# Attention items joined to 512 columns, one compressed item for all groups, and the output projection begun inside the last items

## The chip, the cores and the metric

The kernel runs on one core of a Trainium2 chip. The metric is device microseconds (us) for one execution, the median of several.

## The reference, cut to what matters

Three transformer layers run one after the other on 512 tokens of width 1024, all in float32. The third layer mixes two branches, a gated recurrence (`hgrn2`) and sparse attention (`nsa`), and only `nsa` and the projection behind it are touched here.

```python
# q: 2 kv groups G x 4 query heads R x 512 tokens x 64
s = einsum('bgrtd,bgnd->bgrtn', q, k_cmp) * scale          # 31 compressed keys
p_cmp = softmax(where(cvalid, s, NEG)) * any_valid
o_cmp = einsum('bgrtn,bgnd->bgrtd', p_cmp, v_cmp)
...                                                        # o_slc: keys k_s, causal
...                                                        # o_win: keys k_w, causal
o = gates[..., 0:1]*o_cmp + gates[..., 1:2]*o_slc + gates[..., 2:3]*o_win
mix = concatenate([o_hg, o_nsa]) @ w_out
x = x + gt1 * mix
```

With 512 tokens, 8 blocks and 16 to be selected, the selected branch is plain causal attention, and so is the window branch.

## The kernel before, in words

Every engine has its own program, and semaphores order them; `at(engine, stage, ...)` is the count that an earlier `tick(...)` of the same name reached. The stage of this change is "nsa". It begins with norms and rotations of seven chunks of queries and keys (`ss`, `rotate`; `NORMED` lists the chunks), with the compression of keys and values into 31 (`compress`, 64 products of 62 x 256, then "hidT" and "cmp2"), and with the half of the output projection that needs only `hgrn2` (`ahead(n)`, eight blocks of four 128x512 products, added to the residual by `dve_ahead`).

Then comes the item loop. `ITEMS` lists 36 items: for each query head r (0 to 3; both kv groups g go together) the compressed branch (b = 0), then for b = 1 and 2 the four 128-row query blocks i, each with (i + 1) x 128 keys. Per item TensorE computes scores, transposes the probabilities, and multiplies with the values:

```python
for n, (r, b, i) in enumerate(ITEMS):
    if n + 2 < len(ITEMS):
        scores(n + 2)          # L3466, compressed L3462
    for g in range(NG): ...    # transposes of item n: L3503, compressed L3501
    if n:
        values(n - 1)          # L3482, compressed L3478
```

VectorE runs `front(n + 1)` (masking and row maxima, L3611; compressed L3600 to L3606) and then the scaling of item n (reciprocal of the sum and gate, L3660 and L3664; compressed L3649 to L3656). ScalarE runs `exp(n + 1)` (L3547) and then copies the transposed probabilities of item n from PSUM to SBUF (L3562, L3560). VectorE copies the finished output of a head (`dve_o`, L3683 and L3684). Score banks alternate between the pairs (0, 1) and (6, 7); `scores(n + 2)` waits for `exp(n)`, the transposes of item n wait for its scaling, and `values(n)` for the copies.

Behind the loop `pe_mix_out` does the second half of the output projection, for the left 256 tokens (c = 0) and then the right (c = 1), eight blocks n of four 128x256 products each (L486); it begins only when every engine has ended the stage before (`begin`). VectorE adds each block to the residual (`residual`, L564). The up-projection of the feed-forward net (L675) and the down-projection (L759) follow until the end. Weights come through a ring of slots of 2 MB, loaded by SyncE when TensorE has `used` a slot.

Of the kernel before, what the change touches and what calls it, by code (L numbers as in the profile page):

```python
# [90 lines left out]
def program(nc, dr, out, plan):  # L91
# [3 lines left out]
    with ExitStack() as ctx:  # L95
# [28 lines left out]
        def at(*name):  # L124
            return plan.get(name, 1)
# [350 lines left out]
        def pe_mix_out(pe):  # L476

            tag = "mix_out"
            begin(pe, "pe", tag)
            for c, cols in enumerate(HALVES):  # L480
                for n in range(KC):
                    if n >= 2:
                        pe.wait_ge(dve_done, at("dve", tag, "res", c, n - 2))
                    bank = B[6 * c + n % 2]
                    for k in range(4, KC):
                        last = nc.tensor.matmul(bank[:, cols], out_weights(pe, tag, n, k), HT[:, k, cols], start=(k == 4), stop=(k == KC - 1))  # L486
                    last.then_inc(pe_done, PE.tick(tag, "proj", c, n))
                    if c == 1 and n == 1:
                        pe_mix_sums(pe, 0)
            used((tag, 1))  # L490

# [61 lines left out]

        def dve_mix_out(dve):
# [4 lines left out]

            def residual(c, n):  # L560

                cols = HALVES[c]
                dve.wait_ge(pe_done, at("pe", tag, "proj", c, n))
                nc.vector.scalar_tensor_tensor(out=XT[:, n, cols], in0=B[6 * c + n % 2][:, cols], scalar=mod[:, 2, 16 + n:17 + n], in1=XT[:, n, cols],  # L564
                                               op0=ALU.mult, op1=ALU.add).then_inc(dve_done, DV.tick(tag, "res", c, n))
# [19 lines left out]
            for n in range(KC):  # L585
                residual(0, n)
                if n == 4:
                    first()
                if n == 6:
                    second()  # L590
                add_square(0, n)
            dve_combine(dve, 5, 2, 32, 24, None)
            for n in range(KC):
                residual(1, n)
                if n >= 3:
                    normed(0, n - 3)
                add_square(1, n)
# [2755 lines left out]
        HID = region(o, 4, 2 * NCMP); o += 8 * NCMP  # L3353
        assert o <= 4 * HH * T
# [11 lines left out]
        ITEMS = [(r, b, i) for r in range(4) for b, i in [(0, 0)] + [(b, i) for b in (1, 2) for i in range(NT)]]  # L3366
# [8 lines left out]
        def pe_nsa(pe):  # L3375
# [45 lines left out]
            for n in range(LAST):  # L3421
                ss(n + 1)
                compress(12 * n, 12 * n + 6)
                if n in MIX_AHEAD:
                    ahead(MIX_AHEAD[n])
                rotate(n)
                compress(12 * n + 6, 12 * n + 12)
# [11 lines left out]
            pe.wait_ge(dve_done, at("dve", "nsa", "rotated", LAST - 1))  # L3439
            ahead(KC - 1, 0, 2)  # L3440
            pe.wait_ge(act_done, at("act", "nsa", "hid"))
            for g in range(NG):
                blk = slice(g * NCMP, (g + 1) * NCMP)
                for hc in range(2):
                    nc.tensor.matmul(B[4][half(g), 0:NCMP], w2c[:, 0, hc, :], HID[:, hc, blk], start=(hc == 0), stop=(hc == 1))
                for hc in range(2):
                    last = nc.tensor.matmul(B[5][0:NCMP, g * ND:(g + 1) * ND], HID[:, 2 + hc, blk], w2c[:, 1, hc, :],
                                            start=(hc == 0), stop=(hc == 1))
            last.then_inc(pe_done, PE.tick("nsa", "cmp2"))
            rotate(LAST)  # L3450

            def scores(n):

                r, b, i = ITEMS[n]
                if n == 0:
                    pe.wait_ge(act_done, at("act", "nsa", "cmp2"))
                if n >= 2:
                    pe.wait_ge(act_done, at("act", "nsa", "exp", n - 2, 1))
                if b == 0:
                    for i in range(NT):  # L3460
                        for g in range(NG):
                            last = nc.tensor.matmul(B4[SB[n % 2][g]][:, i, 0:NCMP], NX[half(g), r, i * P:(i + 1) * P], KCMP[half(g), 0:NCMP],  # L3462
                                                    start=True, stop=True)
                else:
                    for g in range(NG):
                        last = nc.tensor.matmul(B[SB[n % 2][g]][:, 0:(i + 1) * P], NX[half(g), r, i * P:(i + 1) * P],  # L3466
                                                NX[half(g), 5 + b, 0:(i + 1) * P], start=True, stop=True)
                last.then_inc(pe_done, PE.tick("nsa", "score", n))

            def values(n):  # L3470

                r, b, i = ITEMS[n]
                pe.wait_ge(act_done, at("act", "nsa", "pt", n, 1))
                if b == 0:
                    if r:
                        pe.wait_ge(dve_done, at("dve", "nsa", "o", r - 1))
                    for g in range(NG):
                        last = nc.tensor.matmul(B[4 + g][half(g), :], VCMP[0:NCMP, g, :], PTn[n % 2][0:NCMP, g, :], start=True, stop=True)  # L3478
                else:
                    for j in range(i + 1):  # L3480
                        for g in range(NG):
                            last = nc.tensor.matmul(B[4 + g][half(g), i * P:(i + 1) * P], VSW[:, j, (b - 1) * P + g * ND:(b - 1) * P + (g + 1) * ND],  # L3482
                                                    PTn[n % 2][:, g, j * P:(j + 1) * P], start=False, stop=True, skip_group_check=True)
                last.then_inc(pe_done, PE.tick("nsa", "pv", n))

            scores(0)
            scores(1)
            ahead(KC - 1, 2, 4)
            for n, (r, b, i) in enumerate(ITEMS):
                if n + 2 < len(ITEMS):  # L3490
                    scores(n + 2)
                for g in range(NG):
# [6 lines left out]
                    for j in range(NT if b == 0 else i + 1):  # L3499
                        if b == 0:  # L3500
                            last = nc.tensor.transpose(B4[2 + g][0:NCMP, j, :], Pn[n % 3][:, 4 * g + j, 0:NCMP], ident[:, :])  # L3501
                        else:
                            last = nc.tensor.transpose(B4[2 + g][:, j, :], Pn[n % 3][:, 4 * g + j, :], ident[:, :])  # L3503
                    last.then_inc(pe_done, PE.tick("nsa", "pt", n, g))
                if n:
                    values(n - 1)
            values(len(ITEMS) - 1)
            PE.mark("end", "nsa")

        def act_nsa(act):  # L3510
# [10 lines left out]
            for kv in (1, 0):  # L3521
# [6 lines left out]
            act.wait_ge(pe_done, at("pe", "nsa", "cmp2"))  # L3528
            nc.scalar.activation(KCMP[:, 0:NCMP], B[4][:, 0:NCMP], ACT.Copy).then_inc(act_done, AC.tick())
            nc.scalar.activation(VCMP[0:NCMP, :, :], B[5][0:NCMP, 0:2 * ND].rearrange("p (g d) -> p g d", g=2), ACT.Copy)\  # L3530
                .then_inc(act_done, AC.tick("nsa", "cmp2"))

            def exp(n):

                r, b, i = ITEMS[n]
                if n >= 3:
                    act.wait_ge(pe_done, at("pe", "nsa", "pt", n - 3, 1))
                if b == 0:
                    for g in range(NG):
                        act.wait_ge(dve_done, at("dve", "nsa", "max", n, g))  # L3540
                        nc.scalar.activation(Pn[n % 3][:, 4 * g:4 * g + 4, 0:NCMP], B4[SB[n % 2][g]][:, :, 0:NCMP], ACT.Exp, scale=SCALE)\
                            .then_inc(act_done, AC.tick("nsa", "exp", n, g))
                else:
                    for g in range(NG):
                        act.wait_ge(dve_done, at("dve", "nsa", "max", n, g))
                        c = 2 * (n % 2) + g
                        nc.scalar.activation(Pn[n % 3][:, 4 * g:4 * g + i + 1, :].rearrange("p j c -> p (j c)"), B[SB[n % 2][g]][:, 0:(i + 1) * P],  # L3547
                                             ACT.Exp, scale=-1.0, bias=small[:, 20 + c:21 + c], accum_out=small[:, 40 + c:41 + c])\
                            .then_inc(act_done, AC.tick("nsa", "exp", n, g))

            exp(0)
            for n, (r, b, i) in enumerate(ITEMS):
                if n + 1 < len(ITEMS):
                    exp(n + 1)
                if n >= 2:
                    act.wait_ge(pe_done, at("pe", "nsa", "pv", n - 2))
                for g in range(NG):
                    act.wait_ge(pe_done, at("pe", "nsa", "pt", n, g))
                    if b == 0:
                        ins = nc.scalar.activation(PTn[n % 2][0:NCMP, g, :], B[2 + g][0:NCMP, :], ACT.Copy)  # L3560
                    else:
                        ins = nc.scalar.activation(PTn[n % 2][:, g, 0:(i + 1) * P], B[2 + g][:, 0:(i + 1) * P], ACT.Copy)  # L3562
                    ins.then_inc(act_done, AC.tick("nsa", "pt", n, g))
            AC.mark("end", "nsa")

        def dve_nsa(dve):
# [22 lines left out]
            cm = cmask[:, :, 0:NCMP]  # L3589
            valid = cmask[:, :, 31:32].rearrange("p i o -> p (i o)")  # L3590

            def front(n):

                r, b, i = ITEMS[n]
                dve.wait_ge(pe_done, at("pe", "nsa", "score", n))
                if b == 0:
                    S = [B4[SB[n % 2][g]][:, :, 0:NCMP] for g in range(NG)]
# [414 lines left out]
```

## Time and profile before

| | |
|---|---|
| time, median of 3 runs | 2637.63 us (2636.24 to 2637.93) |
| the profiled execution's own time | 2635.95 us |
| its span, first to last instruction | 2634.2 us |
| TensorE busy | 2573.3 us, 98% |
| VectorE, ScalarE busy | 1684.4 us (64%), 723.4 us (27%) |
| item loop, first score to last value | 2105.08 to 2199.47 us |

Times of the trace are us from the start of the span. A float32 product appears as two records (a transpose as one), so "x8" of products is four of them. The duration of one record holds its latency; what it costs in a row of others is read from start to start.

### The profile page before, as it was taken

Reading aid. Unit: us, or ns where it says so; the run is one execution under the profiler, and the core shown is the slowest. Engines: PE = TensorE matmul, PEld = TensorE weight load, DVE = VectorE, ACT = ScalarE, POOL = GpSimd, SP = SyncE. Lnnn points to the kernel's source line nnn. Section 1 sums busy time; section 2 is a strip of 40 time slices with the busy share of each in tenths; the row PEclk is TensorE's granted clock in tenths of the full one; section 3 lists DMA queues with packets and bytes.
Section 4 is the critical chain, followed back from the end, with each engine's and each line's share of the span. In section 5 each row is a group of like instructions: output and inputs, shape, how many; then the busy total and the mean of one; then the engine's idle time right before and its main releaser. Section 6 shows DMA issues by size and latency. Waiting matters only on the chain.

```text
span 2634.2 us, 32114 instructions
## 1 busy us (share of the span) xinstructions
PE 2573.3 (98%) x12546; PEld 2061.6 (78%) x12546; DVE 1684.4 (64%) x3035; ACT 723.4 (27%) x1408; POOL 256.2 (10%) x186
## 2 busy tenths in 40 slices
PE   7999999999999999999999999999999999999999
PEld 3888887588888878888888888885445457888888
DVE  3788886687766374555648777645375586666652
ACT  3455553311110022211103111004263365222200
POOL 1333331010000030000001000002121000000000
PEclk9999999999999999999999999999999999999999
DMA  8221311235434321122023454331021310122121
GB/s 348 98 83 73 132 72 65 96 128 192 169 134 155 134 76 68 65 72 96 33 97 128 160 192 153 130 118 67 32 82 64 128 65 33 65 96 96 66 89 54
DMA packets 26373, 276.95 MB, mean 105 GB/s; under 512 B 3688, under 2 KB 4584, under 8 KB 9200
## 3 DMA queue, kind: packets, MB, share of 16 engines
q1 hardware_dynamic: 23040, 269.11, 27.0%
q10 hardware_dynamic: 3184, 5.78, 0.7%
q8 instruction: 101, 1.65, 0.3%
q14 instruction: 48, 0.39, 0.0%
HBM read 272.77 MB, written 2.11 MB: 104 GB/s over the span
## 4 chain that ended last, share of the span: by engine, by line
PE 88%; DVE 7%; ACT 2%; DMA 1%; issue 1%; POOL 0%; SPq 0%; ACTq 0%; DVEq 0%; POOLq 0%
PE bank L675 29%; PE bank L759 15%; PE bank L2585 11%; PE bank L1449 5%; PE bank L2998 5%; PE bank L2371 4%; PE bank L419 3%; PE bank L2676 1%; PE bank L1593 1%; DMA arena<-w_ada 1%; DVE arena L1910 1%; PE bank L486 1%; PE bank L2991 1%; PE bank L1585 1%; PE bank L3466 1%
## 5 line engine op out<-in xcount | busy, mean ns | idle before, releaser
L675 PE MATMUL bank<-HT,ring 128*128 128x256 f32 x1056 | 248.1, 381 | 2.0 <-ACT HT L1091 2.0
L675 PE MATMUL bank<-arena,ring 128*128 128x256 f32 x1056 | 249.6, 380 | 0.0
L675 PE MATMUL bank<-arena 128*128 128x256 f32 x1056 | 249.5, 380 | 0.0
L675 PEld LDWEIGHTS bank<-HT,ring 128*128 128x128 f32 x1056 | 199.8, 190 | 33.7 <-issue 5.2
L675 PEld LDWEIGHTS bank<-arena,ring 128*128 128x128 f32 x1056 | 201.1, 190 | 26.8
L675 PEld LDWEIGHTS bank<-arena 128*128 128x128 f32 x1056 | 201.1, 190 | 26.8
L759 PE MATMUL bank<-arena,ring 128*128 128x256 f32 x936 | 206.9, 380 | 1.4 <-ACT arena L832 1.4
L759 PEld LDWEIGHTS bank<-arena,ring 128*128 128x128 f32 x936 | 177.8, 190 | 26.6 <-ACT arena L832 2.6
L1315 ACT ACTIVATE arena<-bank,ffc 128x512 f32<-128x512 f32 x66 | 51.3, 777 | 485.5 <-DVE bank L1221 485.5
L1120 POOL TENSOR_SCALAR XT<-XT,comb_v 128x512 f32<-128x512 f32 x32 | 50.1, 1577 | 1054.5 <-ACT HT L1091 657.3
L2998 PE MATMUL bank<-HT,ring 128*128 128x512 f32 x320 | 146.5, 598 | 0.5 <-ACT HT L1132 0.5
L1449 PE MATMUL bank<-arena,ring 128*128 128x256 f32 x512 | 130.1, 381 | 1.9 <-DVE arena L1968 0.8
L675 PE MATMUL bank<-HT,arena 128*128 128x256 f32 x528 | 125.6, 381 | 2.7 <-DVE arena L1276 2.6
L759 PE MATMUL bank<-arena 128*128 128x256 f32 x528 | 116.4, 379 | 0.0
L675 PEld LDWEIGHTS bank<-HT,arena 128*128 128x128 f32 x528 | 99.8, 190 | 18.7 <-DVE arena L1276 5.8
L2585 PE MATMUL bank<-arena,ring 128*128 128x256 f32 x512 | 112.7, 380 | 0.3 <-DVE arena L2791 0.3
L759 PEld LDWEIGHTS bank<-arena 128*128 128x128 f32 x528 | 100.6, 190 | 13.4
L2585 PEld LDWEIGHTS bank<-arena,ring 128*128 128x128 f32 x512 | 97.4, 190 | 15.1 <-issue 1.4
L394 DVE SCALAR_TENSOR_TENSOR arena<-ring,evec,arena 128x512 f32<-128x512 f32 x140 | 104.6, 747 | 2.6
L2998 PEld LDWEIGHTS bank<-HT,ring 128*128 128x128 f32 x320 | 57.4, 190 | 58.8 <-issue 56.7
L1231 DVE SCALAR_TENSOR_TENSOR arena<-bank,ffc,arena 128x511 f32<-128x511 f32 (+1 forms) x132 | 98.5, 746 | 3.5 <-ACT arena L1315 1.1
L1449 PEld LDWEIGHTS bank<-arena,ring 128*128 128x128 f32 x512 | 89.2, 191 | 11.5 <-DVE arena L1968 1.2
(514 smaller groups left out, 4598.7 us busy)
## 6 DMA issues: line engine op xcount, KB each, us to landing
ring<-w_ada SPq DMA_DIRECT2D x33, 2048.0 KB, 7.8
ring<-w_up SPq DMA_DIRECT2D x33, 2048.0 KB, 7.7
ring<-w_down SPq DMA_DIRECT2D x24, 1408.0 KB, 6.0
ring<-w_gdn SPq DMA_DIRECT2D x7, 2048.0 KB, 10.1
ring<-w_ret_qk SPq DMA_DIRECT2D x4, 2048.0 KB, 7.9
ring<-w_ret_v SPq DMA_DIRECT2D x4, 2048.0 KB, 7.9
ring<-w_ret_g SPq DMA_DIRECT2D x4, 2048.0 KB, 8.0
ring<-w_ret_out SPq DMA_DIRECT2D x4, 2048.0 KB, 7.9
```

Of the source, the lines that this page charges most:

```text
L394: ins = nc.vector.scalar_tensor_tensor(out=acc, in0=w[:, :, k, :], scalar=evec[:, e, k:k + 1], in1=acc, op0=ALU.mult, op1=ALU.add)
L419: ins = nc.tensor.matmul(B[bank][:, :], out_weights(pe, tag, n, k), src(k), start=(first and k == k0), stop=(last and k == k1 - 1))
L486: last = nc.tensor.matmul(bank[:, cols], out_weights(pe, tag, n, k), HT[:, k, cols], start=(k == 4), stop=(k == KC - 1))
L675: last = nc.tensor.matmul(out_, w[:, k, :], x[:, k, :], start=(first and k == 0), stop=(k == 3), skip_group_check=not first)
L759: last = nc.tensor.matmul(out_, w[:, k, :], x(k), start=(first and k == 0), stop=(k == KH2 - 1), skip_group_check=not first)
L1120: nc.gpsimd.tensor_scalar(XT[:, n, :], XT[:, n, :], comb_v[:, 2, n:n + 1], comb_v[:, 3, n:n + 1], ALU.mult, ALU.add)\
L1231: last = nc.vector.scalar_tensor_tensor(out=out_[:, m:], in0=src[:, 0:T - m], scalar=ffc[:, i, j, half, 2 - m:3 - m], in1=out_[:, m:], op0 ...
L1315: nc.scalar.activation(ffn_y[:, j % 2, :], up_bank(j)[:, :], ACT.Identity, scale=ffc[:, i, j, 0, 2:3], bias=ffc[:, i, j, 0, 3:4])\
L1449: last = nc.tensor.matmul(out_, w[:, k, :], x[:, k, :], start=(first and k == 0), stop=(k == 3), skip_group_check=not first)
L2371: last = nc.tensor.matmul(out_, w[:, k, :], x[:, k, :], start=(first and fresh and k == 0), stop=(k == 7), skip_group_check=not (first and ...
L2585: last = nc.tensor.matmul(out_, left, right, start=flag, stop=(k == 3), skip_group_check=not (first and fresh))
L2998: last = nc.tensor.matmul(bank[:, :], w[:, u, k, :], HT[:, k, :], start=(k == 0), stop=(k == KC - 1))
```

## The change

The item list is new: an item now has always 512 score columns. `FULL_1` and `FULL_2` are query block 3 with its 512 keys; a mixed item joins two parts in one bank, blocks 0 and 2 of one branch (`MIXED_1`, `MIXED_2`: 128 + 384 columns) or blocks 1 of both branches (`MIXED`: 256 + 256). That is 5 items a head. The compressed branch is one item for all four heads: each head and query block takes 31 of 32 columns, so that its probabilities are transposed as four full blocks per group; its values are kept at four partition offsets (`VCMP`, written by "cmp2" four times over). The values of the compressed branch still are one product per group and head. There are 21 items.

Around the loop: `scores(0)` stands before the last rotation and "cmp2", `scores(1)` and `ahead(7)` behind it; within the six steps of norms `rotate` stands before the whole of `compress`; ScalarE takes over one of the two output copies of a head; the left half of the last head's output is copied as soon as the items of blocks 0 to 2 are done, and the first two blocks of the left half of the projection stand before the last item's values, without a wait for the end of the stage.

```diff
-        ITEMS = [(r, b, i) for r in range(4) for b, i in [(0, 0)] + [(b, i) for b in (1, 2) for i in range(NT)]]
+        FULL_1, FULL_2 = ((1, 3, 0),), ((2, 3, 0),)
+        MIXED_1, MIXED, MIXED_2 = ((1, 0, 0), (1, 2, 1)), ((1, 1, 0), (2, 1, 2)), ((2, 0, 0), (2, 2, 1))
+        CMP = ("compressed",)
+        ITEMS = [(0, FULL_1), (0, MIXED_1), (None, CMP), (0, MIXED), (0, MIXED_2), (0, FULL_2)]
+        ITEMS += [(r, parts) for r in range(1, 4) for parts in (MIXED, MIXED_1, MIXED_2, FULL_1, FULL_2)]
+        LEFT_DONE = N_ITEMS - 3
...
+                if parts == CMP:
+                    pe.wait_ge(act_done, at("act", "nsa", "cmp2"))
                     for i in range(NT):
+                        for r in range(4):
+                            for g in range(NG):
+                                last = nc.tensor.matmul(cmp_scores(n, g)[:, 4 * i + r, :], NX[half(g), r, i * P:(i + 1) * P], KCMP[half(g), 0:NCMP],
...
+                    for b, i, o in parts:
...
+                if r and n == FIRST_OF[r]:
+                    pe.wait_ge(dve_done, at("dve", "nsa", "o", r - 1))
+                    pe.wait_ge(act_done, at("act", "nsa", "o", r - 1))
+                    compressed_values(r, True)
...
+            for n in range(N_ITEMS):
+                if n + 2 < N_ITEMS:
+                    if n == 1:
+                        pe.wait_ge(dve_done, at("dve", "nsa", "rotated", LAST))
+                    scores(n + 2)
+                turned(n)
                 if n:
                     values(n - 1)
-            values(len(ITEMS) - 1)
+            pe_mix_proj(pe, 0, 0)
+            pe_mix_proj(pe, 0, 1)
+            values(N_ITEMS - 1)
...
+                if r and n == FIRST_OF[r] + 1:
+                    act.wait_ge(pe_done, at("pe", "nsa", "pv", LAST_OF[r - 1]))
+                    copied(1, r - 1, slice(0, T)).then_inc(act_done, AC.tick("nsa", "o", r - 1))
+                if n == N_ITEMS - 1:
+                    act.wait_ge(pe_done, at("pe", "nsa", "pv", LEFT_DONE))
+                    copied(0, 3, HALVES[0])
+                    copied(1, 3, HALVES[0]).then_inc(act_done, AC.tick("nsa", "left"))
...
+                if n == 0:
+                    scaled(0)
+                    front(1)
+                    dve_ahead(dve, "mix_out", 2, KC - 1, MIX_BANK[KC - 1])
                 else:
-                    c = 40 + 2 * (n % 2)
...
+                    if n + 1 < N_ITEMS:
+                        front(n + 1)
+                    scaled(n)
```

TensorE's program between "hidT" and the loop: before, L419 is `ahead(7)` in two halves, L3445 and L3447 "cmp2", L3418 the last rotation, L3462 and L3466 the first scores.

```order
L3435 MATMUL bank<-ident,arena 128x62 x8
L419 MATMUL bank<-arena,ring 128x512 x2
L3445 MATMUL bank<-arena,w2c 64x31 x2
L3447 MATMUL bank<-w2c,arena 31x64 x2
L3445 MATMUL bank<-arena,w2c 64x31 x2
L3447 MATMUL bank<-w2c,arena 31x64 x2
L3418 MATMUL bank<-arena,rot 128x512
L3462 MATMUL bank<-arena 128x31 x8
L3466 MATMUL bank<-arena 128x128 x2
L419 MATMUL bank<-arena,ring 128x512 x2
L3466 MATMUL bank<-arena 128x256 x2
L3501 MATMUL bank<-ident,arena 31x128 x8
```

Now the same place: L3461 is the rotation, L3553 and L3556 "cmp2", L3500 and L3495 the scores, L3514 the transposes.

```order
L3480 MATMUL bank<-ident,arena 128x62 x8
L3500 MATMUL bank<-arena 128x512 x2
L3461 MATMUL bank<-arena,rot 128x512
L3553 MATMUL bank<-arena,w2c 64x31 x2
L3556 MATMUL bank<-w2c,arena 31x64 x8
L3553 MATMUL bank<-arena,w2c 64x31 x2
L3556 MATMUL bank<-w2c,arena 31x64 x8
L3500 MATMUL bank<-arena 128x128 x2
L3500 MATMUL bank<-arena 128x384 x2
L419 MATMUL bank<-arena,ring 128x512 x4
L3495 MATMUL bank<-arena 128x31 x32
L3514 MATMUL bank<-ident,arena 128x128 x8
```

The first scores moved ahead of "cmp2", whose second product comes 16 times in place of 4, and all 32 compressed score products stand in one piece.

VectorE behind the scores of the compressed item, now: L3674 to L3681 is the compressed item's front, L3713 and L3718 the scaling of the item before it, L3686 the next item's front, L3696 to L3709 the compressed item's scaling.

```order
L3674 TENSOR_TENSOR bank<-bank,cmask 128x16x31 x2
L3677 TENSOR_REDUCE small<-bank 128x16 x2
L3681 TENSOR_TENSOR bank<-bank,small 128x16x31 x2
L3713 RECIPROCAL small<-small 128x4
L3718 TENSOR_SCALAR arena<-arena,small 128x128
L3718 TENSOR_SCALAR arena<-arena,small 128x384
...
L3696 TENSOR_REDUCE small<-arena 128x16 x2
L3698 RECIPROCAL small<-small 128x32
L3701 TENSOR_TENSOR small<-small,cmask 128x16 x2
L3705 TENSOR_TENSOR small<-small,arena 128x16 x2
L3709 TENSOR_TENSOR arena<-arena,small 128x16x31 x2
```

Before, each head had such a front and scaling a quarter as wide (L3600 `128x4x31`), with the scaling of the item before behind it in the same way.

TensorE at the end of the loop, before (L486 is the projection behind the loop):

```order
L3503 MATMUL bank<-ident,arena 128x128 x6
L3482 MATMUL bank<-arena 64x128 x4
L3503 MATMUL bank<-ident,arena 128x128 x8
L3482 MATMUL bank<-arena 64x128 x14
L486 MATMUL bank<-HT,ring 128x256 x40
```

and now (L3541 the values, L501 the projection):

```order
L3514 MATMUL bank<-ident,arena 128x128 x8
L3541 MATMUL bank<-arena 64x128 x8
L3514 MATMUL bank<-ident,arena 128x128 x8
L3541 MATMUL bank<-arena 64x128 x8
L501 MATMUL bank<-HT,ring 128x256 x8
L3541 MATMUL bank<-arena 64x128 x8
L501 MATMUL bank<-HT,ring 128x256 x32
```

Eight of the forty products of the left half moved ahead of the last values.

## Rows read from the trace of the kernel before

**Rows 1.** The page's first part: busy time of TensorE.

```profile
PE 2573.3 (98%) x12546; PEld 2061.6 (78%) x12546; DVE 1684.4 (64%) x3035; ACT 723.4 (27%) x1408; POOL 256.2 (10%) x186
```

**Rows 2.** Chain that ended last, from 2200 us on, shares by line.

```profile
by line: PE bank L675 61.5%; PE bank L759 30.7%; PE bank L486 6.4%; issue 0.4%; PE bank L496 0.2%; PE bank L498 0.2%; DVE XT L894 0.1%; ACT arena L832 0.1%
```

**Rows 3.** Stretches: length; busy PE, PEld, DVE, ACT, POOL; clock; DMA share; GB/s.

```profile
2149.58:2171.71 22.13, 20.49 (x182) 12.78 (x181) 18.79 (x73) 15.92 (x53) 0.00 (x0) 1.00 0.00 1
2100.74:2204.59 103.85, 93.39 (x762) 57.38 (x763) 79.12 (x294) 66.14 (x213) 0.00 (x0) 0.98 0.11 42
```

**Rows 4.** TensorE in order of time, last head: start, us, line, records.

```profile
2187.13 0.70 PE L3466 MATMUL bank<-arena 64*128 64x256 f32 x4
2187.76 1.09 PE L3503 MATMUL bank<-ident,arena 128*128 128x128 f32 x8
2188.78 0.88 PE L3482 MATMUL bank<-arena 128*64 128x128 f32 x12
2189.59 0.92 PE L3466 MATMUL bank<-arena 64*128 64x384 f32 x4
2190.44 0.44 PE L3503 MATMUL bank<-ident,arena 128*128 128x128 f32 x2
2190.80 1.09 PE L3482 MATMUL bank<-arena 128*64 128x128 f32 x16
2191.83 1.13 PE L3466 MATMUL bank<-arena 64*128 64x512 f32 x4
2192.89 0.66 PE L3503 MATMUL bank<-ident,arena 128*128 128x128 f32 x4
```

**Rows 5.** Waits between 2100 and 2202 us: total, times, longest.

```profile
PEld bank L3503 <- DVE arena L3664: 14.9, 23, 1.3
```

**Rows 6.** TensorE before and at the loop's beginning, in order of time.

```profile
2089.39 3.70 PE L419 MATMUL bank<-arena,ring 128*128 128x512 f32 x8
...
2100.74 1.98 PE L419 MATMUL bank<-arena,ring 128*128 128x512 f32 x4 [0.18 <-DVE arena L3628]
...
2103.00 0.41 PE L3447 MATMUL bank<-w2c,arena 128*31 128x64 f32 x4
2103.34 0.42 PE L3445 MATMUL bank<-arena,w2c 128*64 128x31 f32 x4
...
2105.08 1.08 PE L3462 MATMUL bank<-arena 64*128 64x31 f32 x16
2105.99 0.47 PE L3466 MATMUL bank<-arena 64*128 64x128 f32 x4
2106.39 1.99 PE L419 MATMUL bank<-arena,ring 128*128 128x512 f32 x4
```

**Rows 7.** Two stretches at the loop's beginning, columns as in rows 3.

```profile
2107.00:2111.00 4.00, 2.08 (x8) 0.61 (x6) 3.76 (x17) 1.27 (x6) 0.00 (x0) 1.00 0.44 111
2111.00:2115.00 4.00, 3.80 (x16) 1.71 (x18) 2.65 (x14) 2.25 (x7) 0.00 (x0) 0.61 0.99 420
```

**Rows 8.** VectorE at the second compressed item, in order of time.

```profile
2126.61 0.70 DVE L3611 CUSTOM_DVE_ANT_0 bank<-bank,arena 128x512 f32<-128x512 f32 x1 [0.52 <-PE bank L3466]
...
2128.07 0.87 DVE L3664 TENSOR_SCALAR arena<-arena,small 128x384 f32<-128x384 f32 x2
2128.86 0.48 DVE L3600 TENSOR_TENSOR bank<-bank,cmask 128x124 f32<-128x124 f32 x2
2129.37 0.48 DVE L3603 TENSOR_REDUCE small<-bank 128x4 f32<-128x124 f32 x2
...
2130.47 1.00 DVE L3664 TENSOR_SCALAR arena<-arena,small 128x512 f32<-128x512 f32 x2
2131.39 0.29 DVE L3611 CUSTOM_DVE_ANT_0 bank<-bank,arena 128x128 f32<-128x128 f32 x1
```

**Rows 9.** TensorE at the loop's end, in order of time.

```profile
2197.48 1.96 PE L3482 MATMUL bank<-arena 128*64 128x128 f32 x28
2201.09 17.50 PE L486 MATMUL bank<-HT,ring 128*128 128x256 f32 x80 [1.65 <-issue]
```

More of the change, by code:

```diff
@@ L478, in pe_mix_out @@
             tag = "mix_out"
-            begin(pe, "pe", tag)
-            for c, cols in enumerate(HALVES):
+            begin(None, None, tag)
+            for c in range(2):
                 for n in range(KC):
[L482 to L487, printed above, removed]
+                    if c or n >= 2:
+                        pe_mix_proj(pe, c, n)
                     if c == 1 and n == 1:
@@ L3438, in pe_nsa @@
             last.then_inc(pe_done, PE.tick("nsa", "hidT"))
[L3439 to L3448, printed above, removed]
@@ L3468, in scores @@
-                last.then_inc(pe_done, PE.tick("nsa", "score", n))
[L3470 to L3484, printed above, removed]
@@ L3498, in pe_nsa @@
                         pe.wait_ge(act_done, at("act", "nsa", "pt", n - 1, g))
[L3499 to L3503, printed above, removed]
-                    last.then_inc(pe_done, PE.tick("nsa", "pt", n, g))
+                    for j in range(NT):
+                        last = nc.tensor.transpose(B4[2 + g][:, j, :], Pn[n % 3][:, 4 * g + j, :], ident[:, :])
@@ new lines, in turned, with compressed_values, values @@
+                    last.then_inc(pe_done, PE.tick("nsa", "pt", n, g))
+            def compressed_values(r, first):
+                for g in range(NG):
+                    last = nc.tensor.matmul(B[4 + g][half(g), :], VCMP[cmp_rows(r), g, :], PTC[cmp_rows(r), g, :], start=first, stop=True,
+                                            skip_group_check=not first)
+                return last
+            def values(n):
+                r, parts = ITEMS[n]
+                pe.wait_ge(act_done, at("act", "nsa", "pt", n, 1))
+                if parts == CMP:
+                    compressed_values(0, False).then_inc(pe_done, PE.tick("nsa", "pv", n))
+                    return
+                if n == LEFT_DONE + 1:
+                    pe.wait_ge(act_done, at("act", "nsa", "left"))
+                if r and n == FIRST_OF[r]:
+                    pe.wait_ge(dve_done, at("dve", "nsa", "o", r - 1))
+                    pe.wait_ge(act_done, at("act", "nsa", "o", r - 1))
+                    compressed_values(r, True)
+                for m, (b, i, o) in enumerate(parts):
+                    for j in range(i + 1):
+                        for g in range(NG):
+                            first = n == 0 and m == 0 and j == 0
+                            last = nc.tensor.matmul(B[4 + g][half(g), i * P:(i + 1) * P], VSW[:, j, (b - 1) * P + g * ND:(b - 1) * P + (g + 1) * ND],
+                                                    PTn[n % 2][:, g, (o + j) * P:(o + j + 1) * P], start=first, stop=True, skip_group_check=not first)
+                last.then_inc(pe_done, PE.tick("nsa", "pv", n))
@@ new lines, in pe_nsa @@
+            pe.wait_ge(act_done, at("act", "nsa", "std", LAST))
+            pe.wait_ge(dve_done, at("dve", "nsa", "rotated", LAST - 1))
+            scores(0)
+            rotate(LAST)
+            pe.wait_ge(act_done, at("act", "nsa", "hid"))
+            for g in range(NG):
+                blk = slice(g * NCMP, (g + 1) * NCMP)
+                for hc in range(2):
+                    nc.tensor.matmul(B[4][half(g), 0:NCMP], w2c[:, 0, hc, :], HID[:, hc, blk], start=(hc == 0), stop=(hc == 1))
+                for r in range(4):
+                    for hc in range(2):
+                        last = nc.tensor.matmul(B[5][cmp_rows(r), g * ND:(g + 1) * ND], HID[:, 2 + hc, blk], w2c[:, 1, hc, :],
+                                                start=(hc == 0), stop=(hc == 1))
@@ L3505, in pe_nsa @@
+            last.then_inc(pe_done, PE.tick("nsa", "cmp2"))
+            scores(1)
+            ahead(KC - 1)
+            for n in range(N_ITEMS):
[4 more added lines that the diff above has]
+                turned(n)
                 if n:
                     values(n - 1)
-            values(len(ITEMS) - 1)
+            pe_mix_proj(pe, 0, 0)
+            pe_mix_proj(pe, 0, 1)
```

228 lines of the change are left out of this document (128 added, 100 removed).

## The prediction

> **What bounds the kernel now.** I read the page's first part, then the chain of waits behind the changed stage, then stretches of the stage, then its instructions one by one. TensorE is busy 98% of the span [rows 1]. Behind 2200 us the chain is TensorE's own in 98.6% (the two feed-forward products and L486) [rows 2], so whatever TensorE reaches earlier at the projection is earlier at the end, one to one. Inside the item loop it is different: a head takes 22.13 us, of which TensorE is busy 20.49, VectorE 18.79, ScalarE 15.92 [rows 3]. No engine is full; what TensorE waits for is mostly the scaled probabilities, 14.9 us seen from the weight loads [rows 5], part of it covered by products still running. These are handoffs: an item of 128 columns gives TensorE about 1.1 us of work, while masking, exponential and scaling of the next one are still on their way.
>
> I compare from 2100.74, where TensorE is released by the rotation of the sixth chunk [rows 6], to the third block of the projection. That block starts two twentieths into the 80 records of L486, whose 17.50 us began at 2201.09 with 1.65 us of idleness ahead [rows 9]: 16 records are 3.5 us, so 2204.59. The stretch is 103.85 us now [rows 3]. Before 2100.74 the change only swaps `rotate` and parts of `compress`, the same instructions on a TensorE that is busy there; I cost it at nothing. The price if that cover fails is what a late weight slot would cost: the first `compress` slot is released about 5 us later, which I take as at most 1 us.
>
> **Unit costs, from start to start.** Scores of a pair of groups: 0.40 us for 128 columns [rows 6], 0.63 for 256, 0.85 for 384, 1.06 for 512 [rows 4]. Eight transposes 1.02; sixteen records of values 1.03, twelve 0.81 [rows 4]. The compressed values of a head stream as many columns as sixteen such records: 1.03. Four records of "cmp2" 0.34, sixteen of compressed scores 0.91, eight of `ahead` 3.6 (3.70 with the last one's latency) [rows 6].
>
> **What goes and what comes.** Joining leaves the score products as they are (5.9 us a head), and packs transposes and values into full runs: 5 x 1.02 and 5 x 1.03. A head is then 5.9 + 5.1 + 5.15 + 1.03 = 17.2 us of TensorE. The compressed transposes of four heads become those of one item (1.02). VectorE loses three quarters of the compressed item's instructions, 3 of 8 reciprocals a head and one output copy, ScalarE gets that copy (about 0.6) but makes 10 copies of probabilities in place of 18: by rows 8 a mixed item takes VectorE its front (two 256 pairs or 128 + 384, which I put at 1.45, a little over the 1.26 of the 512 pair), 0.2 for the reciprocal and 1.3 for the scaling, 2.95 us, and a full one 1.26 + 0.2 + 0.92 = 2.4: 13.7 a head with 0.7 for the copy 14.4. (2126.61 to 2128.07 is the 512 pair with the reciprocal, 1.46; 2130.47 to 2131.39 the 512 scaling.) ScalarE stays under its 15.92 of now. So TensorE with 17.2 is the fullest engine, with a sixth to spare on the others, and the handoff is shorter than an item: scores of item n + 2 take 1.25 us, its front and the scaling of n + 1 another 2.95, g = 0 of it 0.65 less, so they are there 3.7 us after the iteration's start, while TensorE comes to those transposes only after 3.3 + 1.25 = 4.5. I expect the waits inside a head to vanish.
>
> **The sum.**
> (a) Lead-in. First scores 1.06, rotation 1.0, "cmp2" 0.7 + 8 x 0.34 = 3.4, scores of item 1 1.25, `ahead(7)` 3.6, compressed scores 4 x 0.91 = 3.65: 14.0 us, to 2114.7. The copies of ScalarE and front and scaling of item 0 lie under `ahead(7)`.
> (b) The knot. VectorE does the front of the compressed item ahead of the scaling of item 1. Three pairs of 496 columns have no row; the 124-wide pairs take 0.51 [rows 8], the 512-wide custom pair 1.26. I take 1.3 each, 3.9 us; the lower end (0.5 each) saves 2.4, and a four-dimensional pattern at twice the cost would add 3.9. Then reciprocal and half the scaling, 0.9: transposes of item 1 start near 2119.7, where TensorE would have been ready at 2117.0. Its second group, values of 0 and scores of 4 bring it to 2123.1. VectorE meanwhile needs front of 3 (1.45), sums 1.3, reciprocal 0.2, four small products 0.7 and the first wide one 0.65: 2124.6 for the compressed transposes. The second group comes 0.65 later, and transposes end at 2125.9. Values 1, scores 5, transposes 3 and the compressed values of head 0 end at 2130.1. So this part is 15.4 us, 4.7 of it waiting.
> (c) The rest: scores of 9 mixed and 6 full items 9 x 1.25 + 6 x 1.06 = 17.6; 17 transposes 17.3; 18 values 18.5; compressed values of three heads 3.1; two blocks of the projection 3.5. Together 60.0.
> (d) Waits at head changes and at the end: 0.5. The last-value copies (two of 0.7) and the 1.65 of idleness behind them [rows 9] are gone, since the projection continues with left blocks that need none of them; that cover is 3.5 us of blocks 2 and 3, and without it the two come back, 3.3.
> (e) TensorE's clock. After 2107 to 2111, where it was busy 2.08 of 4 us, the granted clock averaged 0.61 in the next 4 us, that is mostly the lower level of 1.2 GHz [rows 7], about 1.6 us lost. The knot has as much idleness in one place; half of such a loss would hide in it. I take 1.0, with 0 and 3 as ends.
> Sum 14.0 + 15.4 + 60.0 + 0.5 + 1.0 = 90.9, against 103.85: 12.95 us less. On the profiled execution's 2635.95 us this gives 2623.0; the median of the runs is 1.7 higher, 2624.7.
>
> Two places where a row leaves room. The 0.40 to 1.06 us of scores fit 0.19 + 0.0017 per column, and the 0.19 may be paid by pair or by change of instruction kind; rows 4 can't tell, as each score group stands between others. I take it by pair. TensorEngine Tiling (Array Packing) of the Trainium skill, Key Properties, says that changing the tiling mode drains the array; by that rule a mixed item would pay once, and the sum would be 9 x 0.19 = 1.7 us lower. The four records of "cmp2" at 0.34 all go to one column group. The same page says that tiles work independently; by that the four copies of the compressed values could overlap and up to 2.0 us would go. I keep the rows' price for both.
>
> **The rivals.**
> *The loop is tighter than I think* (0.12). Both prices above are lower, the wide VectorE instructions cheap, the clock holds: 1.7 + 2.0 + 1.0 and some 1 us of the knot, a gain near 18, 2619. For it speaks that the clock was 1.00 in the heads [rows 3].
> *Handoffs stay* (0.20). VectorE works in order, and a front that starts late delays the scaling behind it; in the heads of now 1.6 of 22.13 us pass without TensorE busy although no engine is full [rows 3, 5]. With 0.25 us per item on 18 items and a knot 1.5 longer the gain is 7, 2630.6. Against it is the margin of 0.8 us worked out above.
> *It doesn't do what it says* (0.05). The saved time is given back behind the stage, by weights that come no sooner, or the knot's wide patterns cost double and the clock falls twice: gain under 5, 2634. Against it: 0.4% of the later chain is other than work [rows 2], and the DMA engines are idle in the heads (share 0.00) [rows 3].
> *Slower* (0.04). The clock falls at the knot and does not rise: long runs of transposes and half-array products keep it at 1.2 GHz. Some 13 us of full-speed work that is done at the lower level cost 13 us more and eat the gain; over the whole of (c) it is 60 us, 2685 at worst, near 2645 if it holds for a third. Against it: the same kinds ran at 1.00 in rows 3, and of 4 us at 0.61 the clock came back by itself.
>
> **How the numbers follow.** My case, TensorE full in heads 1 to 3 and a knot of 3 to 7 us, gets the remaining 0.59 and its own range 2621 to 2627.5. To leave no more than 2 in 10 outside I reach to the tight loop at 2619.5 and to the handoffs at 2630.5. A measurement here can tell about 0.2%, 5.3 us, from no change. Faster by more needs a gain above 5.3: all of my case, the tight loop and most of the handoffs, 0.91; within 0.2%: 0.05; slower 0.04.
>
> **What would show it.** Right: heads 1 to 3 take 17 to 17.5 us each in place of 22.13, with waits for L3718 under 0.3 us an item; L501 follows the last transposes without a gap; in one place, behind L3495, TensorE waits for VectorE twice, 2.7 and 1.5 us; the feed-forward part is as long as now. Wrong: a wait in every item, which would be the handoffs; L3556 far from 2.7 us or scores of a mixed item near 1.06; a granted clock under 1.00 over more than 5 us; the third block of the projection not near 2191.6.

## The result, and the profile after

The changed kernel takes 2616.89 us (median of 4 runs, 2613.89 to 2617.78) against 2636.93 us before (median of 4, 2634.66 to 2637.93): a ratio of 0.993, 95% interval 0.9917 to 0.9942, some 20 us. Forecast were a gain of 12.95 us and a time of 2624.7, so the measured time lies below the range of 2619.5 to 2630.5.

The page of the changed kernel, span and busy times, against [rows 1]:

```profile
span 2614.7 us, 31974 instructions
PE 2559.8 (98%) x12546; PEld 2055.9 (79%) x12546; DVE 1673.8 (64%) x2978; ACT 719.8 (28%) x1381; POOL 256.2 (10%) x186
```

TensorE has as many records as before and is busy 13.5 us less in a span that is 19.5 us shorter: most of what was won is busy time, not waiting. Stretches of the changed kernel, columns as in [rows 3]: from the first scores to the third block of the projection, the compressed item, and the two later heads.

```profile
2098.53:2185.10 86.57, 82.92 (x762) 55.91 (x762) 68.68 (x237) 61.88 (x184) 0.00 (x0) 0.98 0.13 50
2110.49:2125.62 15.13, 12.21 (x90) 7.98 (x88) 14.70 (x48) 9.48 (x27) 0.00 (x0) 0.89 0.52 223
2137.34:2154.19 16.85, 16.63 (x157) 11.11 (x157) 14.50 (x56) 14.15 (x44) 0.00 (x0) 1.00 0.01 1
```

The stretch that took 103.85 us [rows 3] takes 86.57: TensorE is busy 10.5 us less and idle 3.65 in place of 10.46. A head takes 16.85 in place of 22.13. TensorE's lead-in, in order of time, against [rows 6]:

```profile
2098.53 1.13 PE L3500 MATMUL bank<-arena 64*128 64x512 f32 x4 [0.18 <-DVE arena L3734]
2099.59 1.13 PE L3461 MATMUL bank<-arena,rot 128*128 128x512 f32 x2
2100.64 0.42 PE L3553 MATMUL bank<-arena,w2c 128*64 128x31 f32 x4
2100.99 0.45 PE L3556 MATMUL bank<-w2c,arena 128*31 128x64 f32 x16
2101.37 0.42 PE L3553 MATMUL bank<-arena,w2c 128*64 128x31 f32 x4
2101.72 0.45 PE L3556 MATMUL bank<-w2c,arena 128*31 128x64 f32 x16
2102.10 1.14 PE L3500 MATMUL bank<-arena 64*128 64x128 f32 x8
2103.17 3.70 PE L419 MATMUL bank<-arena,ring 128*128 128x512 f32 x8
```

Sixteen records of L3556 take 0.38 us from start to start, where four took 0.34 [rows 6]; the mixed scores take 1.07 and not 1.25. The compressed item, then an undisturbed piece, then the compressed values of head 1:

```profile
2111.51 1.13 PE L3500 MATMUL bank<-arena 64*128 64x256 f32 x8
2115.36 1.80 PE L3514 MATMUL bank<-ident,arena 128*128 128x128 f32 x8 [2.71 <-DVE arena L3718]
2117.09 1.98 PE L3541 MATMUL bank<-arena 128*64 128x128 f32 x16
2118.99 1.14 PE L3500 MATMUL bank<-arena 64*128 64x128 f32 x8
2120.34 1.24 PE L3514 MATMUL bank<-ident,arena 128*128 128x128 f32 x8 [0.21 <-DVE arena L3709]
...
2126.69 1.09 PE L3514 MATMUL bank<-ident,arena 128*128 128x128 f32 x8
2127.71 1.09 PE L3541 MATMUL bank<-arena 128*64 128x128 f32 x16
2128.73 1.14 PE L3500 MATMUL bank<-arena 64*128 64x128 f32 x8
...
2137.34 1.07 PE L3520 MATMUL bank<-arena 31*64 31x512 f32 x4 [0.22 <-ACT HT L3612]
```

The wait of 2.71 us is where it was forecast. The second, forecast at 1.5, is 0.21, because transposes and values ahead of it ran at the lower clock and took 1.73 and 1.90 us in place of 1.02 each. The stretches around it, columns as in [rows 7], show the clock:

```profile
2113.00:2115.00 2.00, 0.00 (x0) 0.00 (x0) 1.93 (x6) 1.09 (x2) 0.00 (x0) 1.00 0.98 418
2115.00:2119.00 4.00, 3.64 (x26) 2.88 (x26) 3.94 (x14) 2.48 (x9) 0.00 (x0) 0.57 0.82 352
```

The end, against [rows 9]; no gap is left ahead of the projection.

```profile
2179.40 1.09 PE L3541 MATMUL bank<-arena 128*64 128x128 f32 x16
2180.43 3.72 PE L501 MATMUL bank<-HT,ring 128*128 128x256 f32 x16
2184.08 1.09 PE L3541 MATMUL bank<-arena 128*64 128x128 f32 x16
2185.10 14.08 PE L501 MATMUL bank<-HT,ring 128*128 128x256 f32 x64
```

The 16 records ahead of the last values are two of the eight left blocks, 8 of 32 products; the run of forty counted ahead of the prediction holds the first eight products of the right half too.

### The profile page after: what moved, and what is told of

It is laid out like the page before. It is cut to its first block, busy times and chain, and to the rows that moved or that the text cites. A ratio compares the mean times of both kernels' runs of the same rounds, so it can differ in the third digit from the quotient of the medians.

```text
span 2614.7 us, 31974 instructions
## 1 busy us (share of the span) xinstructions
PE 2559.8 (98%) x12546; PEld 2055.9 (79%) x12546; DVE 1673.8 (64%) x2978; ACT 719.8 (28%) x1381; POOL 256.2 (10%) x186
## 3 DMA queue, kind: packets, MB, share of 16 engines
q8 instruction: 101, 1.65, 0.3%
## 4 chain that ended last, share of the span: by engine, by line
PE 87%; DVE 7%; ACT 2%; DMA 2%; issue 1%; POOL 0%; SPq 0%; ACTq 0%; DVEq 0%; POOLq 0%
PE bank L688 28%; PE bank L772 15%; PE bank L2598 11%; PE bank L1462 5%; PE bank L3011 5%; PE bank L2384 4%; PE bank L419 3%; PE bank L2689 1%; PE bank L1606 1%; DMA arena<-w_ada 1%; DVE arena L1923 1%; PE bank L501 1%; PE bank L3004 1%; PE bank L1598 1%; PE bank L3154 1%
```

## The experiments

My theory after the result: TensorE loses some 0.17 us whenever it changes from one kind of product to another (full array, half of its rows, half of its columns), and products of one kind in different column groups run beside each other. The rival is the prediction's pricing: every product, or every group, has its price wherever it stands. e1, e2, e5, e6, e7 and e8 were executed once each (2616.23, 2617.63, 2626.05, 2620.34, 2623.14 and 2635.67 us); what they show is read from stretches of their traces.

**e1_swap**, `rotate` and `compress` as before:

```diff
+                compress(12 * n, 12 * n + 6)
                 if n in MIX_AHEAD:
                     ahead(MIX_AHEAD[n])
-                    rotate(n)
-                    compress(12 * n, 12 * n + 12)
-                else:
-                    compress(12 * n, 12 * n + 12)
-                    rotate(n)
+                rotate(n)
+                compress(12 * n + 6, 12 * n + 12)
```

> The changed kernel with one thing undone: in each of the six steps of norms, half of the compress products stands before ahead and rotate again, and half behind. The same instructions, but in five steps TensorE changes twice more between full 128x128 products and the 62-column compress products. If a change of kind costs TensorE time (my present theory, about 0.17 us each), a step takes 8.43 us in place of 8.09 from one L3439 to the next, and the stretch from the first L419 block to scores(0) 55.5 + 1.4 to 1.8 = 57 us. If the cost lies in the products themselves, as I priced it in the prediction, the step stays at 8.09 and the swap has nothing to do with the 1.4 us found there.

A step of the changed kernel from one L3439 to the next, then one of e1_swap:

```profile
2068.87 1.12 PE L3439 MATMUL bank<-arena,headsum 128*128 128x512 f32 x2
...
2076.96 1.12 PE L3439 MATMUL bank<-arena,headsum 128*128 128x512 f32 x2
```

```profile
2066.72 1.12 PE L3439 MATMUL bank<-arena,headsum 128*128 128x512 f32 x2
2067.78 1.51 PE L3449 MATMUL bank<-ring,arena 128*62 128x256 f32 x12
2069.22 3.70 PE L419 MATMUL bank<-arena,ring 128*128 128x512 f32 x8
2072.76 1.02 PE L3461 MATMUL bank<-arena,rot 128*128 128x512 f32 x2
2073.71 1.51 PE L3449 MATMUL bank<-ring,arena 128*62 128x256 f32 x12
2075.16 1.12 PE L3439 MATMUL bank<-arena,headsum 128*128 128x512 f32 x2
```

A step takes 8.44 us in place of 8.09, 0.35 more for two changes of kind, 0.17 each. From the first block of L419 to the first scores it is 56.98 us against 55.50, so the 1.4 us ahead of the first scores are the swap. That is 1.48 and not ten times 0.17, because one step of the changed kernel waits 0.20 us for VectorE. The whole time of e1_swap, 2616.23 us, is not longer than that of the changed kernel: the executions differ by more than this ahead of the stage (see below), so the reading rests on the stretch.

**e2_copies**, one column group for the four copies (`cmp_rows(0)` in place of `cmp_rows(r)` in "cmp2"):

> The changed kernel, but the four copies of the compressed values in cmp2 are all written to the same 31 partitions, one after the other, so the compressed values of heads 1 to 3 are read from stale rows (part of the computation is changed). If the four copies were cheap because they went to four column groups of the array that work at the same time, the two groups of 16 records now take 4 x 0.34 = 1.36 us each in place of 0.38, and the cmp2 stretch 3.4 us in place of 1.46. The rival: 0.34 us was never a price per four records but a fixed price of beginning such a group, with the records themselves nearly free; then it stays at 1.46.

TensorE of e2_copies in order of time, the third and fourth copy:

```profile
2100.79 1.08 PE L3556 MATMUL bank<-w2c,arena 128*31 128x64 f32 x16
2101.80 0.42 PE L3553 MATMUL bank<-arena,w2c 128*64 128x31 f32 x4
```

Sixteen records take 1.01 us in place of 0.38, "cmp2" 2.71 in place of 1.46. So the column groups do work beside each other, or at least four copies into four places pass faster than four into one: e2_copies writes one place four times over, and the two were not separated. My 1.36 was too high as well: four records at 0.34 and sixteen at 1.01 are 0.12 for the beginning and 0.056 a record. Of the 1.95 us by which I overpriced "cmp2", 1.25 are the overlap and 0.7 the beginning counted eight times.

**e5_between** and **e6_beside**, the same extra product in two places:

```diff
                     for b, i, o in parts:
+                        if o:
+                            nc.tensor.matmul(B[SB[n % 2][0]][:, o * P:(o + 1) * P], NX[:, 0, 0:P], NX[:, 1, 0:P], start=True, stop=True)
```

```diff
+                    if g == 0 and len(ITEMS[n][1]) == 2:
+                        nc.tensor.matmul(B[2][:, 0:P], NX[:, 0, 0:P], NX[:, 1, 0:P], start=True, stop=True)
                     for j in range(NT):
```

> The changed kernel with one more product (128x128, full array) between the two parts of each of the 12 mixed items' scores, into a place that the second part overwrites. It breaks one run of half-array products in two: two more changes of kind. To be compared with e6_beside. If a change of kind costs 0.15 to 0.19 us, the extra here is the product's 0.12 to 0.2 plus 0.3 to 0.4 us for each mixed item, scores with it 1.55 us in place of 1.07, and a head is 1.5 to 1.8 us longer (three mixed items).

> The changed kernel with the same extra 128x128 product, but ahead of the transposes of each mixed item, which use the full array as it does, and into the place that the first transpose overwrites: no further change of kind. If changes of kind are what costs, an item is longer by the product alone, 0.12 to 0.2 us, a head by 0.4 to 0.6 us. If every separate group of products costs a fixed time whatever its kind, the head is as long as in e5_between.

First e5_between, then e6_beside, both at the second mixed item of head 0:

```profile
2129.57 0.70 PE L3502 MATMUL bank<-arena 64*128 64x256 f32 x4
2130.20 0.49 PE L3500 MATMUL bank<-arena 128*128 128x128 f32 x2
2130.62 0.70 PE L3502 MATMUL bank<-arena 64*128 64x256 f32 x4
2131.26 1.09 PE L3516 MATMUL bank<-ident,arena 128*128 128x128 f32 x8
```

```profile
2128.75 0.49 PE L3514 MATMUL bank<-arena 128*128 128x128 f32 x2
2129.07 1.04 PE L3516 MATMUL bank<-ident,arena 128*128 128x128 f32 x8
2130.04 1.09 PE L3543 MATMUL bank<-arena 128*64 128x128 f32 x16
```

Between the parts the scores take 1.69 us, 0.62 more than 1.07. Beside the transposes both together take 1.29, 0.27 more than 1.02. The same product, 0.35 us apart, for two changes of kind: 0.17 to 0.18 each. A head takes 18.71 and 17.39 us; it is only 0.54 longer in e6_beside, although three products cost 0.8, because the 0.22 us wait for ScalarE's copy is gone there. The product itself was dearer than the 0.12 to 0.2 I expected.

**e4_short**, short items with the one compressed item kept (the transposes and copies go by the item's blocks):

```diff
+        ONE = {(b, i): ((b, i, 0),) for b in (1, 2) for i in range(NT)}
...
+        ITEMS += [(r, ONE[k]) for r in range(1, 4) for k in ((1, 1), (2, 1), (1, 0), (1, 2), (2, 0), (2, 2), (1, 3), (2, 3))]
```

> The changed kernel with short items again: each query block is an item of its own with 128 to 512 columns, eight a head, and only the compressed branch is joined. If it was the joining that took the handoffs away, a head takes 22.13 - 0.9 - 1.0 = 20.2 us in place of 16.85, the loop is 13 us longer and the time near 2630. If the one compressed item did most of it, a head takes 17.5 to 18 us, the time is near 2620. A small part, about 1.3 us a head, comes in both cases from six more changes of kind on TensorE and shows as busy, not as idle.

A later head of e4_short as a stretch, columns as in [rows 3]:

```profile
2135.73:2154.20 18.47, 18.15 (x157) 11.01 (x156) 15.12 (x58) 14.94 (x50) 0.00 (x0) 1.00 0.01 1
```

The time is 2624.93 us (2623.18 to 2627.24, ratio 0.9959, 0.9944 to 0.9974). A head takes 18.47 us with 0.32 of idleness. So short items alone don't make the handoffs late, and of the 5.28 us a head 3.66 came with the compressed branch leaving the heads (and the new order of items), 1.62 with the joining, 1.52 of it busy time. This fits the price of a change of kind: three items fewer are nine changes fewer (scores, transposes, values), not the six I counted, and nine at 0.17 are 1.5 us. The 20.2 us were wrong, and 18.47 is over the 17.5 to 18 of the other case too. Part of the 8 us between the two kernels is not the items: the clock was at the lower level for 5 us and more behind the compressed item here.

**e8_load**, e4_short with VectorE's old burden put back as idle work:

```diff
+                for _ in range(k):
+                    step(nc.vector.tensor_tensor(SINF, SINF, COSF, ALU.mult))
...
+                if r and n == FIRST_OF[r]:
+                    burden(3)
```

> e4_short with VectorE burdened: at the first item of heads 1 to 3, three idle 128x512 operations ahead of its front and three ahead of its scaling, 3.7 us a head, about what the compressed branch of a head cost VectorE before. TensorE's work stays as in e4_short (head of 18.47 us, of which 0.32 waiting). If it was VectorE's load by the compressed branch that made the handoffs late before, the waits come back to 1.5 us or more a head and a head takes 19.7 to 20.5 us. If the handoffs went for another reason (the order of items), the head stays under 19.

TensorE of e8_load in order of time, three groups of transposes of a later head:

```profile
2152.59 1.11 PE L3520 MATMUL bank<-ident,arena 128*128 128x128 f32 x8 [0.32 <-DVE arena L3734]
2156.61 1.11 PE L3520 MATMUL bank<-ident,arena 128*128 128x128 f32 x8 [1.47 <-DVE arena L3734]
2160.49 0.76 PE L3520 MATMUL bank<-ident,arena 128*128 128x128 f32 x4 [1.32 <-DVE arena L3734]
```

The waits are back, 3.1 us a head, and a head takes 21.5 us (compressed values at 2142.11 and 2163.64), over what I expected. VectorE is busy 19.08 us of it, near the 18.79 of before [rows 3], yet in the kernel before TensorE stood idle for only 1.6 us a head, so VectorE's total load alone does not set the wait. TensorE does the same work as in e4_short, so VectorE's load in one place is enough to make the handoffs late; that it was all of the cause before is likely, not shown, since the items also stand in another order.

**e3_tail**, the early blocks and their freedom from the stage's end undone:

```diff
-            begin(None, None, tag)
+            begin(pe, "pe", tag)
...
-            pe_mix_proj(pe, 0, 0)
-            pe_mix_proj(pe, 0, 1)
             values(N_ITEMS - 1)
```

> The changed kernel with its tail undone: the first two left blocks of the projection stand behind the last values again, behind a wait for the end of the stage on every engine. By the prediction (two copies and the idleness, 3.3 us less one copy that ScalarE now does at the same time) TensorE stands still for 2.3 to 3.3 us between the last values and L501, and the time is 2619 to 2620.5. The rival: the copies overlap and the wait is under 1.7 us as in the kernel before, 2618.5.

Measured: 2617.97 us (2617.38 to 2619.97, ratio 0.9934, 0.9917 to 0.9951), and 0.67 us of idleness ahead of L501 in the trace. The rival holds. The early blocks are worth some 0.7 us; the rest of the 1.65 us gap of before [rows 9] went because each engine now copies one half of one head only (0.42 and 0.38 us at the same time). In the kernel before, VectorE made both copies within that gap, which lasted to 2201.09:

```profile
2199.49 0.68 DVE L3683 COPY HT<-bank 64x512 f32<-64x512 f32 x1 [2.83 <-PE bank L3482]
2200.19 0.69 DVE L3684 COPY HT<-bank 64x512 f32<-64x512 f32 x1
```

**v1_scaled** and **v2_scaled**, VectorE's order at the compressed item:

```diff
+                elif n == 1:
+                    scaled(n)
+                    front(n + 1)
```

(v2_scaled: `elif n in (1, 2)`.)

> The changed kernel with one order changed on VectorE: the scaling of item 1 stands ahead of the front of the compressed item, in the 2.9 us in which VectorE waited for the compressed scores. The 2.71 us wait of TensorE ahead of the transposes of item 1 should go; the compressed transposes then wait for VectorE's front of item 3 and the compressed scaling, about 2 us. From the transposes of item 0 to the compressed values of head 0 it should take 13.3 us in place of 15.1, the time 2615.1 (2616.9 now). If the clock falls as before (0.57 over 4 us in the changed kernel) and less of it hides behind a wait, only 0.5 us is won.

> As v1_scaled, and the compressed item's own scaling also stands ahead of the front of item 3. The compressed transposes come 1.4 us earlier at the earliest, the same stretch takes 12.4 us, the time is 2614.2. The rival: the front of item 3, now 3.5 us later, makes TensorE wait ahead of the transposes of item 3 for as long, and v2 equals v1.

v1_scaled: 2617.78 us (2613.67 to 2618.27, ratio 0.9931, 0.9919 to 0.9944); the stretch takes 15.08 us, nothing is won. The 2.71 us went, the wait ahead of the compressed transposes became 2.57, and the fall of the clock behind it now lay in the open. v2_scaled: 2616.13 us (2615.82 to 2617.50, ratio 0.993, 0.9916 to 0.9943); the stretch takes 14.31 us, where I expected 12.4. Two things came on top. One is the rival: TensorE waits 1.13 us ahead of the scores of item 5, for the exponentials of item 3. The other is the clock, some 1.6 us. It fell earlier, with no wait ahead, as TensorE of v2_scaled in order of time shows:

```profile
2107.21 3.76 PE L3495 MATMUL bank<-arena 64*128 64x31 f32 x64
2110.90 1.77 PE L3514 MATMUL bank<-ident,arena 128*128 128x128 f32 x8
2112.60 2.08 PE L3500 MATMUL bank<-arena 64*128 64x256 f32 x8
```

By their times neither kernel can be told from the changed one.

**e7_narrow**, the narrow products done twice:

> The changed kernel with each of the 32 compressed score products done twice, so that TensorE runs 7.4 us of 31-column products without waiting for anything. If such narrow products let the clock fall although TensorE is busy, the granted clock goes below 1.00 within this run or right behind it, earlier than the 2.71 us wait. If only waiting does it, the clock is 1.00 up to that wait and falls behind it as in the changed kernel.

Stretches of e7_narrow in the midst of its narrow products, columns as in [rows 7]:

```profile
2109.00:2111.00 2.00, 2.00 (x41) 2.00 (x40) 0.00 (x0) 0.00 (x0) 0.00 (x0) 1.00 0.67 246
2111.00:2113.00 2.00, 2.00 (x34) 2.00 (x33) 0.00 (x0) 0.00 (x0) 0.00 (x0) 0.81 1.04 442
2113.00:2115.00 2.00, 2.00 (x23) 2.00 (x22) 0.00 (x0) 0.00 (x0) 0.00 (x0) 0.50 1.05 442
```

The run of L3496 lasts from 2107.50 to 2117.05, TensorE waits for nothing, and the clock falls in the midst of it. Here it stayed at 1.2 GHz until about 2126.

**v3_early** and **v4_copy**, the compressed scores ahead of `ahead(7)`, and the copy at a change of head ahead of the exponential:

```diff
             scores(1)
+            scores(2)
             ahead(KC - 1)
...
```

> The changed kernel with the compressed scores ahead of ahead(7) on TensorE, so that its 3.6 us of wide products stand where VectorE works on the compressed front; VectorE does the fronts of items 1 and 2, then the residual of ahead(7), then the scaling of 1, of 2 and the front of 3; ScalarE does the exponential of item 2 ahead of the copies of item 0. By the durations of v2_scaled the waits of TensorE at the compressed item shrink to about 1.5 us from 4.2, and from the scores of item 1 to the compressed values of head 0 it takes 20.0 us in place of 23.5: 2613.4 us. If the fall of the clock comes from the narrow products rather than from waiting, it falls here too, over the wide ones, and 1.7 us of the gain are lost: 2615.

> As v3_early, and at a change of head ScalarE copies its half of the finished output ahead of the next exponential. The three waits of 0.22 us ahead of the compressed values (on ScalarE's copy) should go, 0.7 us in all. The rival: the exponential, 0.6 us later, delays a scaling by as much and the gain is nothing.

v3_early takes 2615.30 us (2614.56 to 2615.77, ratio 0.9926, 0.9913 to 0.9938), v4_copy 2614.37 us (2612.20 to 2616.86, ratio 0.9924, 0.9910 to 0.9937). From the first scores to the third block of the projection it is 85.55 and 84.65 us, against 86.57: 1.0 and 1.9 less. The clock fell behind the narrow products again, over L419, whose eight records took 5.4 us in place of 3.7, as the second half of the expectation had it. From the scores of item 1 to the compressed values of head 0 v3_early takes 22.5 us, over the 20.0 expected, and over 21.7 with the clock's fall. Its clock behind the narrow products, which end at 2107.40, columns as in [rows 7]:

```profile
2107.00:2109.00 2.00, 2.00 (x12) 1.11 (x11) 1.46 (x3) 0.07 (x1) 0.00 (x0) 0.71 0.00 0
2109.00:2111.00 2.00, 2.00 (x4) 0.88 (x3) 1.97 (x4) 0.19 (x1) 0.00 (x0) 0.50 0.00 0
```

In v4_copy the waits of 0.22 us are gone. By their times alone these two can't be told from the changed kernel, since the intervals overlap; the traces say it is 1 to 2 us.

## Why the prediction was wrong

The direction and TensorE as the bound were right, and the waits inside a head went as forecast, though not for the reason given. Three of the signs it had named for being wrong came: L3556 took 0.76 us in place of 2.7, the mixed scores 1.07, and the third block stood at 2185.10, not near 2191.6. By its terms, in the profiled executions:

- (a) lead-in, 14.0 forecast, 11.96 measured (2098.53 to 2110.49). The step that failed is "8 x 0.34" for "cmp2", 1.95 us too much, as e2_copies showed; the rest is the mixed scores of item 1.
- (b) the knot, 15.4 forecast, 15.13 measured. The three wide pairs took 1.3 us each, as priced.
- (e) clock, 1.0 forecast on top. It fell, to 0.57 over 4 us, some 1.6 us lost (1.73 and 1.90 in place of twice 1.02), but all of it lay in (b), where it took the place of the second wait. Of "half of such a loss would hide in it" the half should have been all.
- (c) and (d), 60.5 forecast, 59.48 measured (2125.62 to 2185.10). The step "I take it by pair" failed: mixed scores cost 1.07, 1.6 us less for nine. Against that, the waits took 1.0 where (d) had 0.5 (those of 0.22 for ScalarE's copy are 0.29 each from start to start), and the two blocks 0.15 more.
- "I cost it at nothing": the swap of `rotate` and `compress` gained 1.4 us. I looked only for what it might make late.

The stretch thus gained 17.3 us where 12.95 were forecast, the swap 1.4, and the remaining 0.8 us lie ahead of the stage, in code that is the same. I count them as difference between executions: in the profiled executions of the changed kernel and its variants, all alike up to there, the first block of L419 begins anywhere from 2040.55 to 2044.83. The rules of the Trainium skill that I set aside (TensorEngine Tiling (Array Packing), Key Properties: a change of tiling mode drains the array, different tiles work independently) point the right way in both places: the traces have 0.17 to 0.18 us for a change and 0.38 in place of 1.01 us for four column groups. They show a cost, not what the array does in it. With the two prices right and nothing added for the clock, the sum would have been 4.6 us lower, near 2620, inside the tight-loop rival to which I gave 0.12. The swap and the 0.8 us account for most of the rest.

Of the rest: the waits inside a head vanished, as forecast, but e4_short and e8_load put the reason elsewhere than I did. I had called short items the cause; with VectorE unburdened they pass with 0.32 us of idleness a head. The tail was priced at 3.3 us for its cover, and is worth 0.7: the two copies lie inside the 1.65 us of idleness and should not have been added to it. The slower rival had its place right (the clock falls at the compressed item) and came back by itself, as I argued.

## What to carry to other kernels

Count changes of kind on TensorE (full array, half rows, half columns) as a cost of their own, here 0.17 to 0.18 us each, and group products of one kind, in stages that never wait too. When small items seem to cause handoff waits, look first at the load of the engine that stands between, and test by giving it back. A row whose few records take 0.34 us is no price per record: it holds the group's beginning.

## What the runs showed that I had not expected

The granted clock fell to the lower level (0.50, 1.2 GHz) while TensorE was 100% busy with 31-column products on half of its rows (e7_narrow), or right behind 3.7 us of them (v2_scaled, v3_early); in the changed kernel and in v1_scaled it fell only after the wait that followed. What decides between the two isn't shown: up to the end of those products TensorE does the same in v2_scaled as in the changed kernel. Weights were on their way in e7_narrow (DMA share 0.67 to 1.05), but the fall does not need them, since the share was 0.00 in v3_early. The clock was below 1.00 within 2115 to 2119 in the changed kernel and within 2111 to 2127 in e7_narrow.

Four column groups of 31 columns took 0.38 us for 16 records, one group 1.01.
